# A two-block transformer kernel: a sixth projection unit of the state space branch written as seven half-block products, its taps and the attention mask's additions placed between the units' sums

## The reference

```python
proj = h @ w_in
q_lat, kv_lat, k_idx, w_idx, z, xbc, dt_raw, g_a, g_b = jnp.split(proj, IN_SPLITS, axis=-1)
# sparse attention: 16 heads of 128, two blocks of 128 queries
iscore = jnp.einsum('bqh,bqhs->bqs', w_b, relu(jnp.einsum('bqhd,bsd->bqhs', qi_b, k_idx)))
_, idx = lax.top_k(iscore, k_sel_n)          # 64 of 256 keys
logits = jnp.einsum('bqhc,bqkc->bhqk', q_b, kv_sel) * scale + bias
probs = softmax(where(valid, logits, -inf)); o = probs @ kv_sel
# state space branch: xbc has 4096 channels
xbc = silu(causal depthwise convolution of 4 taps over tokens (xbc) + conv_b)
```

## Time and profile before

| | |
|---|---|
| median of three runs | 1321.97 us (1321.64 to 1322.38) |
| the profiled execution, its own time | 1321.71 us |
| its span (first to last instruction) | 1319.6 us |
| PE, DVE, ACT, POOL busy | 99%, 71%, 32%, 14% |
| granted TensorE clock over the span | 0.999 |

### The profile page before, as it was taken

The page is one execution under the profiler, slowest core; times in us unless marked ns, Lnnn a source line. Parts: engine busy times, 40 slices in busy tenths (PEclk is TensorE's granted clock), DMA queues, the critical chain, the costliest instruction groups (busy, mean ns, idle before and its releaser), DMA issues.

```text
span 1319.6 us, 21693 instructions
## 1 busy us (share of the span) xinstructions
PE 1308.5 (99%) x8989; PEld 1168.0 (89%) x8989; DVE 931.6 (71%) x1576; ACT 419.4 (32%) x912; POOL 186.5 (14%) x171
## 2 busy tenths in 40 slices
PE   9999999999999999999999999999999999999998
PEld 7985899988898599998877899999999986999987
DVE  3975798657587388857872898887887845865653
ACT  2154333220216333323055425454732103100101
POOL 2300322030200032205033000003100100011100
PEclk9999999999999999999999999999999999999999
DMA  9632567676523257767639843146645454545550
GB/s 318 203 128 96 192 249 263 217 269 218 187 99 128 96 193 270 254 225 270 211 86 251 246 131 114 32 154 223 200 129 187 168 188 129 190 148 174 176 174 33
DMA packets 129409, 238.18 MB, mean 180 GB/s; under 512 B 7413, under 2 KB 34317, under 8 KB 128801
## 3 DMA queue, kind: packets, MB, share of 16 engines
q1 hardware_dynamic: 123354, 218.26, 48.1%
q0 software_dynamic: 5552, 18.34, 5.1%
q10 hardware_dynamic: 407, 0.20, 0.1%
HBM read 231.49 MB, written 6.34 MB: 180 GB/s over the span
## 4 chain that ended last, share of the span: by engine, by line
PE 92%; DVE 4%; DMA 2%; issue 1%; SPq 0%; ACT 0%; DVEq 0%
PE acc L2186 58%; PE scr L2186 17%; PE pvw L2186 9%; DMA ring<-in_w_up 1%; PE ptb L2294 1%; PE scr L2789 1%; PE pvw L2796 1%; DMA hid<-in_x 1%; PE scr L2285 1%; PE ptb L2186 1%; DVE ring L1338 1%; PE pvw L2304 1%; DVE ring L1278 1%; DVE work L1340 1%; DVE work L1337 0%
## 5 line engine op out<-in xcount | busy, mean ns | idle before, releaser
L2186 PE MATMUL acc<-y,ring 128*128 128x128 f32 (+2 forms) x1136 | 163.3, 299 | 0.0
L2186 PEld LDWEIGHTS acc<-y,ring 128*128 128x128 f32 (+1 forms) x1136 | 150.9, 191 | 9.6 <-issue 1.3
L2186 PE MATMUL acc<-x,ring 128*128 128x128 f32 (+1 forms) x832 | 120.7, 299 | 0.0
L2186 PEld LDWEIGHTS acc<-x,ring 128*128 128x128 f32 x832 | 110.9, 192 | 5.8 <-issue 1.0
L2186 PE MATMUL acc<-ring,big 128*128 128x256 f32 (+1 forms) x376 | 115.5, 453 | 0.0
L2186 PEld LDWEIGHTS acc<-ring,big 128*128 128x128 f32 x376 | 70.6, 190 | 33.3 <-issue 26.9
L2186 PE MATMUL acc<-ring,hid 128*128 128x256 f32 (+1 forms) x364 | 98.8, 417 | 0.0
L888 ACT ACTIVATE ring<-ring,silc 128x512 f32<-128x512 f32 x96 | 60.1, 709 | 92.3 <-DMA ring<-in_ada_w 92.3
L2186 PEld LDWEIGHTS acc<-ring,hid 128*128 128x128 f32 x364 | 68.4, 190 | 21.7 <-issue 14.3
L2186 PE MATMUL acc<-ysq,ring 128*128 128x128 f32 x592 | 71.9, 275 | 0.1
L2186 PEld LDWEIGHTS acc<-ysq,ring 128*128 128x128 f32 x592 | 68.9, 192 | 0.4 <-ACT ysq L1070 0.4
(11 more groups left out here) (573 smaller groups left out, 2787.8 us busy)
## 6 DMA issues: line engine op xcount, KB each, us to landing
ring<-in_w_in SPq DMA_DIRECT2D x24, 2048.0 KB, 9.3
ring<-in_w_up SPq DMA_DIRECT2D x16, 2048.0 KB, 8.7
ring<-in_w_down SPq DMA_DIRECT2D x16, 2048.0 KB, 8.0
ring<-in_ada_w SPq DMA_DIRECT2D x12, 2048.0 KB, 12.8
ring<-in_w_ffn_in SPq DMA_DIRECT2D x22, 1024.0 KB, 7.3
ring<-in_w_out SPq DMA_DIRECT2D x6, 2048.0 KB, 7.9
ring<-in_w_o_ssd SPq DMA_DIRECT2D x4, 2048.0 KB, 8.6
ring<-in_w_ffn_out SPq DMA_DIRECT2D x4, 2048.0 KB, 8.1
```

The source lines that it names most:

```text
L2186: ins = pe.matmul(dst, w, m, start=start, stop=stop, is_transpose=turned, skip_group_check=True)
```

## The change

P2 becomes a seven unit (`SEVEN_XBC` from 5 to 6, and so `FIRST_SEVEN` from 3 to 2). Four banks of plain units are left, b2 = 0 to 3. On DVE the taps of banks 2 and 3 (`conv2(2)`, `conv2(3)`) now stand between the sums of P2, and the four mask additions, which all stood ahead of the first seven unit, now stand: one in P3 ahead of `xbc_combine`, and one at the end of each of P3, P4 and P5.

```diff
-SEVEN_XBC = 5
+SEVEN_XBC = 6
 FIRST_SEVEN = 16 // 2 - SEVEN_XBC
 ...
-                act.activation(pre[:, b2 % 2, :, TAPS2 - 1:], b[:, :, :], ACT.Copy).then_inc(drained, 3 if last else 1)
-                act.wait_ge(drained, DONE + bank[0] + 2 * last)
+                act.activation(pre[:, b2 % 2, :, TAPS2 - 1:], b[:, :, :], ACT.Copy).then_inc(drained, 5 if last else 1)
+                act.wait_ge(drained, DONE + bank[0] + 4 * last)
 ...
             for b2 in range(2 * FIRST_SEVEN):

-                if b2:
+                if b2 in (1, 2):
                     conv2(b2 - 1)
                 if b2 in (0, 1):
                     select(b2)
-                if 2 <= b2 < 6:
-                    mask_bias((b2 - 2) // 2, b2 % 2)
 ...
                     if j == 0:
                         xbc_sums(u)
-                        if u:
+                        if u == 0:
+                            conv2(2)
+                        else:
+                            if u == 1:
+                                mask_bias(0, 0)
                             xbc_combine(u - 1)
                     elif j == 1:
                         if u:
                             other_taps(u - 1, 0)
-                        else:
-                            conv2(2 * FIRST_SEVEN - 1)
                     elif j == 2:
                         xbc_late_sums(u)
-                    elif u:
+                    elif u == 0:
+                        conv2(3)
+                    else:
                         other_taps(u - 1, 1)
+                        if u < 4:
+                            mask_bias(u // 2, u % 2)
             xbc_combine(SEVEN_XBC - 1)
 ...
-                ins.then_inc(filled, 3 if b2 == 2 * FIRST_SEVEN - 1 else 1)
+                ins.then_inc(filled, 5 if b2 == 2 * FIRST_SEVEN - 1 else 1)
```

More of the change, by code:

```diff
@@ L1043, in _ @@
                 last = b2 == 2 * FIRST_SEVEN - 1
-                act.activation(pre[:, b2 % 2, :, TAPS2 - 1:], b[:, :, :], ACT.Copy).then_inc(drained, 3 if last else 1)
-                act.wait_ge(drained, DONE + bank[0] + 2 * last)
+                act.activation(pre[:, b2 % 2, :, TAPS2 - 1:], b[:, :, :], ACT.Copy).then_inc(drained, 5 if last else 1)
+                act.wait_ge(drained, DONE + bank[0] + 4 * last)
                 for i in range(2):
                     first_tap(2 * b2 + i, pre[:, b2 % 2, i, 0:T])
-            bank[0] += 2
+            bank[0] += 4
             act.activation(acum[:, :, :], full()[:, :, 0:SSD_HEADS], ACT.Copy).then_inc(drained, 2)
```

## The result

The changed kernel takes 1324.41 us (median of 15 runs, 1324.05 to 1325.50), against 1321.93 us of the kernel before (15 runs, 1321.52 to 1323.26). That is **2.5 us slower**: a ratio of 1.0018, interval 1.0011 to 1.0025. The forecast was 1322.8 with a range to 1324.3. The sign was right, the time lies just outside the range, and the loss is three times as large as forecast.

The account below looks back on a forecast made before the run. PE bounds the kernel: busy for 99% of the span, 92% of the chain that ended last. Waits of 1.6 + 0.6 less 1.37 saved give +0.8 us on the median of 1321.97: 1322.8 us, range 1320.5 to 1324.3.

Parts of the forecast that it names:

- PE saves 1.37 us: P2 on PE: a seven unit takes 12.50 us against 13.87 for a plain one, so 1.37 us shorter.
- DVE owes 7.3 us more: P2 on DVE: two pairs of sums and the combining add 2.40 + 2.40 + 2.50 = 7.3 us of new work.
- PE waits at the transposes of steps 1 and 2: P4 on PE: waits for DVE's attention weights, 1.6 us at step 1 and 0.6 us at step 2, with no third wait.
- The sum of these, +0.8: Whole kernel: waits of 1.6 + 0.6 less 1.37 saved, some 0.4 us either way.
- So P2 itself costs no wait: P2 on PE, from 765.31 to 777.81: its sums and fourth plain bank are there before PE needs them, so no wait.
- on a bank in P2: P2 on PE: a wait on a bank there was listed as showing the forecast wrong; no size was given.
- DVE's chain from 782.85: P3 on DVE: `other_taps` starts at about 782.85 after ACT's first taps, and DVE is solid from there.
- (a): Rival on DVE's queue: it packs better than start-to-start times say, so the 1.37 us stays whole, 1320.6 us; chance 0.18.
- (b): Rival in the attention loop: DVE comes X later than walked and PE pays X at step 1; over 0.2% slower, chance 0.08.
- X = 1.8 us: DVE's extra lateness from which (b) decides: a first tap at 784.7 rather than 782.9.
- (c): Rival on PE's clock: it falls to 1.2 of 2.4 GHz after the 1.6 us hole, costing 1.85 us, 1324.7; chance 0.03.
- (d): Rival on PE in P2: the seven unit is no shorter than a plain one, sum +2.2, or 1324.2; chance 0.03.

Follow-up runs that it names:

- e1: The changed kernel, with the running sums' product waiting for the drain of the bank it takes instead of the count; 1322.97 us against 1321.95 before.
- e5: The kernel before, with only a wait for the last plain bank's drain added ahead of the running sums' product; 1323.18 us against 1321.70 before.
- e7: The changed kernel, with all four mask additions moved ahead of P2's first sums; 1327.09 us against 1321.70 of the kernel before.
- e4: The changed kernel, with the running sums' own-bank wait, first mask addition behind the combining and second in P4; 1320.86 us against 1321.95 before.

## Why the prediction was right and wrong

**Right.** PE saves 1.37 us. DVE owes 7.3 us more and cannot pay it in P3. PE waits at the transposes of steps 1 and 2, for 1.6 and 0.6 us (measured 1.66 and 0.52), and at no later step. The sum of these, +0.8, is near to what e1 gives (+1.04) where the other cause is away.

**Wrong: the step "So P2 itself costs no wait".** It placed P2's start one plain unit earlier, at 765.31, and looked at `ready(38)` alone for a bank. The product of the running sums ahead of P2 and its `free_bank()` are in no step of the walk, so this wait stood in the sum at nothing. The larger increments (3 to 5, 2 to 4) were taken for book-keeping that keeps the later numbers in line. The semaphore sees a count, not a bank. The product waited for the last plain bank's drain, 1.48 us at P2's start. e1 (1.36 us less in the stretch) and e5 (1.02 us more with nothing else changed) show it from both sides. A wait "on a bank in P2" was among the prediction's own signs of being wrong, and that is the sign that came.

**Also missing: the two lags are tied.** A late PE is not a shorter wait at step 1, since DVE's late sums of P2 wait for PE's products. In the prediction DVE's chain from 782.85 was taken as DVE's alone. With the bank wait it starts at 784.25, and in e1, without it, at 782.95. This is also why the forecast 1.6 us at step 1 came out (1.66) in a kernel where PE reached that step 1.4 us later than forecast: DVE was late by as much.

**The rivals.** (a) fell: the move did not hide. (b) named a lateness of DVE in the loop of the steps, with X = 1.8 us; DVE was 1.4 us late, but PE itself was the source, and the time stays under the 1324.6 at which (b) was to begin. (c) is not in the changed kernel: all its windows of 2 us from 736 to 880 us read full clock. But it exists: in e7, behind a wait of 2.87 us, the clock did fall and cost 1.7 us. (d) fell with e4, and in the changed kernel itself P2's 112 records take 12.6 us from start to start, against 13.87 for a plain unit.

**Small slips.** The price of (c), 0.8 + 1.85 on 1321.97, is 1324.6 and not 1324.7; its 3.7 us at the lower level come from no row and are only the length at which it would matter. Of the two idle times "with known cause", the row of the second (1.0 us) names none ("issue"). By the walk's own durations `acc[1]` is needed at 782.3, not 782.0. None of these moves the sum.

## What to carry to other kernels

When a loop is shortened and a semaphore's last increment is enlarged to keep the numbers behind it, work out for each waiter which event now makes the count pass. A count that jumps holds back everyone who needed a value inside the jump.

Where a unit's matrix work falls by 10% for more sums on another engine, compare the two engines unit by unit, not over the whole: here 7.3 us more DVE work cost 2.2 us of PE's time, all of it at the first steps of attention, and none at the steps behind them. Of two orders with the same work, the better one puts a long independent instruction where the engine would wait for another, here for ACT.

## What the hardware showed that was not expected

In e7 PE waited 1.18 us until 767.0 and 2.87 us until 776.2. The granted clock was 0.76 in the 2 us from 776, 0.50 (1.2 of 2.4 GHz) in the next 2 us and 0.89 in the 2 us behind. That cost e7 some 1.7 us on top of its waits. The Trainium skill, "TensorE: Matmul & The Clock Gate", "What's actually happening", says that the clock goes by how busy PE has been lately and has these two levels; e7 agrees, with 0.50 in its window. Whether the first of e7's waits had a part in it, these runs do not tell.

In the traces of before, the change and the other experiments every window of 2 us from 736 to 880 us reads full clock; their longest wait there is 1.57 us (e1). In the changed kernel the windows behind its waits of 1.19 and 1.50 us, 30 us apart, read full clock:

```profile
766.00:768.00 2.00, 2.00 (x18) 2.00 (x19) 1.97 (x4) 1.09 (x3) 0.00 (x0) 1.00 0.28 30
...
798.00:800.00 2.00, 2.00 (x17) 1.92 (x16) 1.97 (x4) 0.93 (x2) 0.00 (x0) 1.00 0.00 0
```
